# The scan of an RWKV-7 layer on one NeuronCore: group norm statistics, their transposition and two sets of products moved in hand-written queues

## The chip, the cores and the metric

The kernel runs on one core of one Trainium2 chip. The metric is the device time of one execution in microseconds (us). The three runs of the kernel before took 3165.90, 3161.59 and 3163.92 us, with a median of 3163.92 us. TensorE is called PE, its weight loads PEld, VectorE DVE, ScalarE ACT, GpSimd POOL, and the queue that issues the weight DMAs SP.

## The reference

Four transformer blocks of width 1024 over 256 tokens (each a feed-forward, a mixer and another feed-forward) are followed by a fifth block of another design. The mixers of the first and of the fourth block are RWKV-7 time mixes; only these two are touched here. Of such a mixer this is the part that matters:

```python
def step(state, inp):
    r_t, w_t, k_t, v_t, kk_t, a_t = inp
    sa = jnp.einsum('bhvk,bhk->bhv', state, -kk_t)
    state = (state * w_t[:, :, None, :]
             + sa[..., None] * (kk_t * a_t)[:, :, None, :]
             + v_t[..., None] * k_t[:, :, None, :])
    return state, jnp.einsum('bhvk,bhk->bhv', state, r_t)
...
_, y = lax.scan(step, state0, (tm(rh), tm(wh), tm(kh), tm(vh), tm(kk), tm(ah)))
mean = jnp.mean(y, axis=-1, keepdims=True)
var = jnp.mean(jnp.square(y - mean), axis=-1, keepdims=True)
y = ((y - mean) * lax.rsqrt(var + RW_GN_EPS)).reshape(bsz, seq, d) * ln_w + ln_b
out = ((y + bonus.reshape(bsz, seq, d)) * g).astype(h.dtype) @ w_o
```

There are 16 heads of 64 channels. All arithmetic is fp32.

## The kernel before

Each engine has its queue written out by hand in program order, and the queues meet in semaphores. Weights are streamed by SP into a ring of three slots; POOL streams the modulation weights into two buffers, which DVE adds up in pieces of 1.0 or 1.8 us (`beside()`, L505) wherever its queue has one; in the second RWKV layer there are none.

The scan over 256 tokens is done in chunks of 128 tokens, by inverting a triangular matrix per head in levels of 16, 32 and 64 tokens. Its work is cut in four units: unit `u` has chunk `b = u // 2` and head half `u % 2`. An iteration `n` of 1, 2, 3 works on two units at once, the inverse of the head unit `n` and the outputs of the tail unit `n - 1`. PE's queue in an iteration is: `near_again(head)`, `rest(tail)`, `turn_y(head)`, `upper(tail)`, from `n = 2` on `turn_out(n - 2)`, the level 16 product, `across(tail)`, `x32`, `lower(tail)`, `y32`, `state_and_out(tail)`, `level32`, `receptances`, `y64`, `keys` in two halves. `rest`, `upper` are the products of L1631, L1635, L1646 and L1651: first those with all 128 rows of the array (`z.kl` as weights), then, for the second chunk alone (units 2 and 3), those with 64 rows (`z.kk`, `z.r` against the carried state). An fp32 product of this kind stands in the trace as two instructions. Most other products are recorded under L323, the helper `mm`.

DVE masks or adds each product: L2146 and L2160 are the masks of `level16` and `level32`, L2151 and L2156 the sums behind `x32` and `y32`, L2164 is the mask behind `receptances`, L2169 the sum behind `y64`, L2175 the mask behind the two halves of `keys`. `y64` on PE waits for L2160, the second half of `keys` for L2169, `rest` for all of L2175.

Then comes the group norm of the tail unit: `centre` on DVE (L2189, L2190, L2191: sum, mean, subtraction), `spread_read` on ACT (L1902: square), `variance` on DVE (L2196), `deviation` on ACT (L1906: root), `normed` on DVE (L2200, L2202: reciprocal, product). `turn_out` on PE (four transpositions) waits for `normed` by the semaphore `wk_gn`; `out_read` on ACT (L1913) scales what it turned, and `gated` on DVE (L2208, L2209) makes the input of the output projection.

In DVE's queue `centre` stands behind `keys`, at the end of the iteration. In ACT's queue `spread_read` and `deviation` of a unit stand one iteration later than its outputs, around `rest_read` and `x_read`.

Behind the third iteration only unit 3 is left. PE fills the gaps between its steps with `early_outputs(0)` to `(7)`, the output projection of the first chunk, sixteen instructions each; `late_outputs` (L1698) is that of the second chunk.

Of the kernel before, what the change touches and what calls it, by code (L numbers as in the profile page):

```python
# [1224 lines left out]
UNITS = 4  # L1225
# [137 lines left out]
def rw_products(k, pe, pr, j, n):  # L1363
    s, z, tiles = k.sem, RwTiles(k), RwOrder(j, pr.q)
    mm, left = pr.mm, iter(rw_order(j))
# [203 lines left out]
    def near_again(c):  # L1569
        near_product(c.u, 0, k.psum[:, c.bank(0)], None)  # L1570
        near_product(c.u, 1, k.psum[:, c.bank(1)], s["wk_near"])
# [53 lines left out]
    def rest(c):  # L1625
        at("wk_rk_read", c, 1, 2)
        if c.b:
            pe.wait_ge(s["wk_state_read"], 2 * j + c.hf + 1)
        for p in range(4):
            for i in range(2):  # L1630
                ins = part(k.psum[:, c.bank(i), p * 64:(p + 1) * 64], lhsT=z.kl[c.hf][:, 4 * i + p, 1],  # L1631
                           rhs=z.vt[:, c.b, 4 * c.hf + p, z.rows(i)], start=p == 0, stop=c.b == 0, skip_group_check=True)
        for p in range(4 if c.b else 0):
            for i in range(2):
                ins = part(k.psum[:, c.bank(i), p * 64:(p + 1) * 64], lhsT=z.kk[z.rows(i), 4 * c.hf + p, z.now(c.b)],  # L1635
                           rhs=z.state[z.rows(i), 4 * c.hf + p], start=False, stop=True, skip_group_check=True)
        ins.then_inc(s["wk_res"], 1)

    def upper(c):
        at("wk_res_read", c)  # L1640
        for m in range(8):
            mm(k.psum[0:64, c.bank(2), m * 64:(m + 1) * 64], z.y[c.hf][0:64, m, 0:64], z.res[c.hf][0:64, m],
               True, True, s["wk_sa"] if m == 7 else None)
        for p in range(4):
            for i in range(2):
                part(c.out(i, p), lhsT=z.kl[c.hf][:, 4 * i + p, 0], rhs=z.vt[:, c.b, 4 * c.hf + p, z.rows(i)],  # L1646
                     start=p == 0 and (c.b == 1 or i == 0), stop=False, skip_group_check=True)
        if c.b:
            for p in range(4):
                for i in range(2):  # L1650
                    part(c.out(i, p), lhsT=z.r[z.rows(i), 4 * c.hf + p, z.now(c.b)],  # L1651
                         rhs=z.state[z.rows(i), 4 * c.hf + p], start=False, stop=False, skip_group_check=True)

    def across(c):
        at("wk_sa_read", c, 0, 2)
        for m in range(8):
            mm(k.psum[64:P, c.bank(3), m * 64:(m + 1) * 64], z.am[c.hf][0:64, m, 64:P], z.sa[c.hf][0:64, m],
               True, True, s["wk_across"] if m == 7 else None)
# [7 lines left out]
    def state_and_out(c):  # L1666
        at("wk_sa_read", c, 1, 2)
        if c.b == 0:
            for p in range(4):
                for i in range(2):  # L1670
                    o = k.psum[z.rows(i), c.bank(0), p * 64:(p + 1) * 64]
                    mm(o, z.ended_t[0][:, 4 * c.hf + p, z.rows(i)], z.sa[c.hf][:, 4 * i + p], True, False)
                    mm(o, z.ended_t[1][:, 4 * c.hf + p, z.rows(i)], z.vt[:, 0, 4 * c.hf + p, z.rows(i)], False, True,
                       s["wk_state"] if p == 3 and i else None)
        for p in range(4):
            for i in range(2):
                ins = part(c.out(i, p), lhsT=z.rb[c.hf][:, 4 * i + p], rhs=z.sa[c.hf][:, 4 * i + p], start=False,
                           stop=True, skip_group_check=True)
        ins.then_inc(s["wk_out"], 1)

    def turn_out(c):
        at("wk_gn", c)
        for p in range(4):
            pr.turn(k.psum[:, c.turned(), p * P:(p + 1) * P], z.yn_pair[:, p], s["wk_out_turned"] if p == 3 else None)

    def early_outputs(d):
        if d == 0:
            pe.wait_ge(s["rw_gated"], UNITS * j + 2)
        for t in range(KT):
            slot, at = divmod(base + d * KT + t, BLOCKS)  # L1690
            if t == 0:
                pe.wait_ge(k.weights_loaded[slot % RING], 16 * (slot // RING + 1))
            mm(k.psum[:, d // 4 * 2, d % 4 * P:(d % 4 + 1) * P], k.weights[:, slot % RING, at * P:(at + 1) * P],
               z.r[:, t, z.now(0)], t == 0, t == KT - 1)
# [26 lines left out]
    for n in range(1, UNITS):  # L1721
        head, tail = units[n], units[n - 1]
        if head.b:
            pe.wait_ge(s["wk_sa_read"], 2 * (UNITS * j + head.u - 1))
        near_again(head)
        rest(tail)
        turn_y(head)
        upper(tail)
        if n >= 2:
            turn_out(units[n - 2])  # L1730
        if n == 1 and j == 0:
            turn_mod_rows(k, pe, pr, 2)
        level16(head)
        across(tail)
        if n == 1 and j == 0:
            pe.wait_ge(s["mod_ready"], 3)
        x32(head)
        lower(tail)
        y32(head)
        state_and_out(tail)  # L1740
        level32(head)
        receptances(head)
        if n == UNITS - 1:
            early_outputs(0)
        y64(head)
        keys(head)
    tail = units[3]
    early_outputs(1)
    rest(tail)
    early_outputs(2)  # L1750
    upper(tail)
    early_outputs(3)
    turn_out(units[2])
    across(tail)
    early_outputs(4)
    lower(tail)
    early_outputs(5)
    state_and_out(tail)
    early_outputs(6)
    early_outputs(7)  # L1760
    pe.wait_ge(s["rw_gated"], UNITS * j + 3)
    for d in range(KT):
# [27 lines left out]
def rw_act(k, act, ev, j, v_first):  # L1790
# [109 lines left out]
    def spread_read(c):  # L1900
        at("wk_spread_in", c)
        act_(z.sq, z.yn, f.Square).then_inc(s["wk_sq"], 1)  # L1902

    def deviation(c):
        at("wk_var", c)
        act_(z.stat[c.hf][:, 1], z.stat[c.hf][:, 1], f.Sqrt, bias=k.const("gn_eps"), scale=1.0 / 64)\  # L1906
            .then_inc(s["wk_deviation"], 1)
# [10 lines left out]
    for n in range(UNITS + 1):  # L1918
        if n < UNITS:
            near_read(units[n])  # L1920
        if n >= 2:
            spread_read(units[n - 2])
        if n:
            rest_read(units[n - 1])
        if n < UNITS:
            x_read(units[n])
        if n >= 2:
            deviation(units[n - 2])
        if n == 0:
            values_read()  # L1930
            ended_read()
        if n:
            upper_read(units[n - 1])
        if n >= 2:
            out_read(units[n - 2])
        if n:
            lower_read(units[n - 1])
            if units[n - 1].b == 0:
                state_read(units[n - 1])
    spread_read(units[3])  # L1940
    deviation(units[3])
    out_read(units[3])


# [26 lines left out]
def rw_vector(k, dve, own, n, j, q0):  # L1971
# [161 lines left out]
    def open_y(c):  # L2133
        if c.b:
            dve.wait_ge(s["wk_sa"], 2 * (UNITS * j + c.u - 1))
        same = k.const("same16").rearrange("p (c t) -> p c t", t=16)
        for m in range(8):
            i, p = divmod(m, 4)
            ins = v.tensor_tensor(z.y[c.hf][:, m].rearrange("p (c t) -> p c t", t=16),
                                  z.base[:, c.u, 4 * (1 - i) + p:4 * (1 - i) + p + 1].to_broadcast([P, 8, 16]),  # L2140
                                  same, mult)
        ins.then_inc(s["wk_open"], 1)
# [15 lines left out]
    def level32(c):  # L2158
        at("wk_lx", c, 1, 2)
        v.tensor_tensor(z.t[c.hf], c.pair(1), each("level5"), mult).then_inc(s["wk_t"], 1)  # L2160
# [24 lines left out]
    def centre(c):  # L2185
        at("wk_out", c)
        if c.u:
            dve.wait_ge(s["wk_out_turned"], UNITS * j + c.u)
        own.of(v.tensor_reduce(stat(c, 0), c.outs(), AX.X, add))  # L2189
        own.of(v.tensor_scalar(z.stat[c.hf][:, 0], z.stat[c.hf][:, 0], 1.0 / 64, None, mult))  # L2190
        v.tensor_tensor(z.yn, c.outs(), stat(c, 0).unsqueeze(3).to_broadcast([P, 2, 4, 64]), sub)\  # L2191
            .then_inc(s["wk_spread_in"], 1)
# [40 lines left out]
    for n in range(1, UNITS):  # L2233
        head, tail = chunks[n], chunks[n - 1]
        if n == 1 and j == 0:
            mod_columns(k, dve, own, 2)
        level16(head)
        across(tail)
        x32(head)
        y32(head)  # L2240
        beside()
        if n >= 2:
            gated(chunks[n - 2])
        if n + 1 < UNITS:
            open_y(chunks[n + 1])
        level32(head)
        receptances(head)
        y64(head)
        keys(head, 0)
        keys(head, 1)  # L2250
        centre(tail)
        variance(tail)
        normed(tail)
        beside(2)
# [1406 lines left out]
```

## Time and profile before

| | |
|---|---|
| median of three runs | 3163.92 us |
| time of the profiled execution | 3165.9 us |
| its span | 3164.1 us |
| instructions | 49803 |
| PE busy | 3044.1 us, 96% |
| DVE busy | 2373.9 us, 75% |
| ACT busy | 1399.7 us, 44% |
| chain that ended last | PE 85%, DVE 10%, ACT 2%, DMA 2%, issue 1% |
| mean granted TensorE clock | 0.978 |

The span is the time from the first to the last instruction in the profiled execution; the time of a run is a little longer than it. The share of an engine says how long it was occupied in the whole program. The chain that ended last says which engine each moment waited for, followed back from the last instruction. The scan units of the first RWKV layer lie at 419 to 543 us of the span, those of the second at 2306 to 2433 us.

### The profile page before, as it was taken

What the parts mean: (1) busy time and instruction counts of PE and PEld (TensorE: products, weight loads), DVE (VectorE), ACT (ScalarE), POOL (GpSimd) and SP (SyncE); (2) the same over time, 40 slices, a digit from 0 to 9 for tenths busy, and PEclk for the clock granted to TensorE, in tenths of its full rate; (3) what the DMA queues carried; (4) which work ended last, traced back from release to release, by engine and by line L of the source; (5) the groups of instructions that cost most, each with busy time, mean ns of one, the idle gap of its engine ahead of it and who ended that gap; (6) DMA issues with size and microseconds to landing.
All of it is one profiled execution on the core that took longest, in us unless ns stands there. A gap on an engine that the chain in (4) does not pass through costs nothing.

```text
span 3164.1 us, 49803 instructions
## 1 busy us (share of the span) xinstructions
PE 3044.1 (96%) x19866; PEld 2679.8 (85%) x19866; DVE 2373.9 (75%) x3501; ACT 1399.7 (44%) x2222; POOL 97.0 (3%) x187
## 2 busy tenths in 40 slices
PE   7998999999999999999999999999989999999998
PEld 6886789888888988888886888887788888989887
DVE  6978865988877867878867887877754866765685
ACT  4534121544545753545444554534122544465453
POOL 0000000000000000000000000000000000000000
PEclk9999999999999999999999999999999999999899
DMA  8774423676676336675764666662301553443453
GB/s 349 252 287 150 155 100 109 247 269 254 244 264 224 118 119 230 245 283 204 265 236 151 240 260 231 245 244 100 114 1 61 197 183 125 170 167 140 160 182 132
DMA packets 69670, 609.47 MB, mean 193 GB/s; under 512 B 7728, under 2 KB 7888, under 8 KB 31824
## 3 DMA queue, kind: packets, MB, share of 16 engines
q1 hardware_dynamic: 42768, 459.41, 39.1%
q0 software_dynamic: 26352, 144.88, 12.2%
q8 instruction: 158, 2.59, 0.3%
q10 hardware_dynamic: 336, 2.13, 0.2%
q14 instruction: 56, 0.46, 0.0%
HBM read 604.30 MB, written 2.10 MB: 192 GB/s over the span
## 4 chain that ended last, share of the span: by engine, by line
PE 85%; DVE 10%; ACT 2%; DMA 2%; issue 1%; SPq 0%; DVEq 0%; POOLq 0%; ACTq 0%
PE psum L323 26%; PE psum L926 23%; PE psum L930 12%; PE psum L947 10%; PE psum L954 6%; PE psum L321 4%; PE psum L951 2%; PE psum L1698 1%; DVE ada_sum L505 1%; DMA weights<-in_weights 1%; DVE arena L812 1%; DMA ada_in<-in_ada_w 1%; DVE arena L2307 1%; DVE wkv_base L2075 1%; DVE small L2074 1%
## 5 line engine op out<-in xcount | busy, mean ns | idle before, releaser
L877 ACT ACTIVATE unit_high<-weights 128x1024 fp32r<-128x1024 f32 x594 | 628.6, 1060 | 704.7 <-PE psum L930 388.2
L883 DVE TENSOR_TENSOR unit_low<-weights,unit_high 128x1024 fp32r<-128x1024 f32 x594 | 725.5, 1223 | 197.7 <-ACT unit_high L877 197.2
L926 PE MATMUL psum<-h_part,unit_high 128*128 128x512 f32 x3168 | 821.1, 396 | 21.0 <-DVE h_part L799 14.7
L926 PEld LDWEIGHTS psum<-h_part,unit_high 128*128 128x128 f32 x3168 | 576.6, 191 | 129.6 <-issue 17.1
L930 PEld LDWEIGHTS psum<-h_part,unit_low 128*128 128x128 f32 x3168 | 445.6, 192 | 29.5
L930 PE MATMUL psum<-h_part,unit_low 128*128 128x256 f32 x3168 | 466.9, 284 | 0.0
L323 PE MATMUL psum<-in_part,w_part 128*128 128x256 f32 x2784 | 361.3, 290 | 7.2 <-issue 4.8
L323 PEld LDWEIGHTS psum<-in_part,w_part 128*128 128x128 f32 x2784 | 348.4, 196 | 23.1 <-issue 10.8
L947 PE MATMUL psum<-hidden,unit_high 128*128 128x512 f32 x1386 | 353.7, 396 | 0.0
L1053 DVE TENSOR_REDUCE arena<-psum 128x256 f32<-128x512 f32 x396 | 272.7, 689 | 59.1 <-PE psum L930 47.6
L505 DVE SCALAR_TENSOR_TENSOR ada_sum<-ada_in,c_act,ada_sum 128x1536 f32<-128x1536 f32 x154 | 278.6, 1812 | 25.4 <-DMA ada_in<-in_ada_w 25.2
L947 PEld LDWEIGHTS psum<-hidden,unit_high 128*128 128x128 f32 x1386 | 249.2, 189 | 44.2
L323 PE MATMUL psum<-arena,weights 128*128 128x256 f32 (+4 forms) x1360 | 274.2, 374 | 6.6 <-DVE arena L1947 4.3
L323 PEld LDWEIGHTS psum<-arena,weights 128*128 128x128 f32 (+3 forms) x1360 | 216.9, 190 | 60.2 <-issue 27.5
L323 PE MATMUL psum<-arena 128*128 128x128 f32 (+6 forms) x2112 | 231.8, 280 | 22.5 <-DVE arena L2056 7.3
L323 PEld LDWEIGHTS psum<-arena 128*128 128x128 f32 (+3 forms) x2112 | 194.7, 171 | 55.5 <-issue 14.6
L1173 DVE TENSOR_TENSOR w_part<-weights,w_part 128x1024 fp32r<-128x1024 f32 x144 | 175.2, 1221 | 87.6 <-ACT w_part L1167 87.0
L954 PEld LDWEIGHTS psum<-hidden,unit_low 128*128 128x128 f32 x1584 | 214.7, 190 | 13.9
L954 PE MATMUL psum<-hidden,unit_low 128*128 128x256 f32 x1584 | 221.1, 282 | 0.0
L1167 ACT ACTIVATE w_part<-weights 128x1024 fp32r<-128x1024 f32 x144 | 150.9, 1050 | 16.4 <-PE psum L323 16.4
L489 POOL DMA_DIRECT2D ada_in<-in_ada_w x180 | 95.0, 528 | 1976.2 <-DVE ada_sum L505 1461.1
L1018 ACT ACTIVATE hidden<-arena 128x256 fp32r<-128x256 f32 x198 | 82.8, 418 | 89.5 <-DVE arena L1089 73.4
(314 smaller groups left out, 2804.7 us busy)
## 6 DMA issues: line engine op xcount, KB each, us to landing
weights<-in_weights SPq DMA_DIRECT2D x290, 1536.0 KB, 6.5
ada_in<-in_ada_w POOLq DMA_DIRECT2D x182, 768.0 KB, 5.9
consts<-in_consts POOLq DMA_DIRECT2D x1, 1700.0 KB, 16.2
x<-in_x SPq DMA_DIRECT2D x1, 1024.0 KB, 9.2
v_first<-arena ACTq DMA_DIRECT2D x1, 1024.0 KB, 5.0
arena<-v_first ACTq DMA_DIRECT2D x1, 1024.0 KB, 4.8
weights<-in_weights SPq DMA_DIRECT2D x1, 512.0 KB, 5.1
out<-x SPq DMA_DIRECT2D x1, 512.0 KB, 2.6
```

The costliest lines, as they stand in the source:

```text
L321: ins = self.k.nc.tensor.matmul(out, lhsT=w, rhs=x, start=start, stop=stop, skip_group_check=True)
L323: ins = self.k.nc.tensor.matmul(out, lhsT=w, rhs=x, start=start, stop=stop, is_transpose=turn)
L505: ins = k.nc.vector.scalar_tensor_tensor(out, buf, c, out, ALU.mult, ALU.add)
L877: k.nc.scalar.activation(k.unit_part[0][:, n % UNIT_RING], w, ACT.Copy).then_inc(k.sem["unit_high"], 1)
L883: k.nc.vector.tensor_tensor(k.unit_part[1][:, n % UNIT_RING], w, k.unit_part[0][:, n % UNIT_RING].bitcast(FP32), ALU.subtract).then_inc(k. ...
L926: mm(k.psum[:, 2 * (j % 2) + half, :].rearrange("p (i t) -> p i t", i=2), lhsT=part(2 * j + half, 0, t), rhs=k.h_parts[:, :, t], start=t = ...
L930: ins = mm(k.psum[:, 2 * (j % 2) + half, 0:T], lhsT=part(2 * j + half, 1, t), rhs=k.h_part[0][:, t], start=False, stop=t == KT - 1, skip_g ...
L947: mm(k.psum[:, out_bank(d), :].rearrange("p (i t) -> p i t", i=2), lhsT=w, rhs=x, start=f == 0, stop=f == FT - 1, skip_group_check=True)
L954: ins = mm(k.psum[:, out_bank(d), 0:T], lhsT=part(UNITS_UP + v, 1, b), rhs=k.hidden_part[f][:, 0], start=False, stop=f == FT - 1, skip_gro ...
L1053: v.tensor_reduce(to[:, j % RING], k.psum[:, 2 * (j % 2) + half, :].rearrange("p (i t) -> p t i", i=2), AX.X, ALU.add).then_inc(k.sem["gat ...
L1167: self.k.nc.scalar.activation(self.k.w_part[0][:, m % RING], w, ACT.Copy).then_inc(self.k.sem["w_high"], 1)
L1173: self.k.nc.vector.tensor_tensor(self.k.w_part[1][:, m % RING], self.weights(m)[1], self.k.w_part[0][:, m % RING].bitcast(FP32), ALU.subtr ...
```

## The change

Five things are moved; no instruction of arithmetic is added or taken away.

- PE: `turn_out(n - 2)` goes from behind `upper(tail)` to the place right behind `near_again(head)`, ahead of `rest(tail)`.
- PE: in `rest` and `upper` of units 2 and 3 the 64-row products of a pair `p` follow right behind its 128-row products, where before all 128-row products came first. `rest` uses the helper `mm`, and each product opens its own columns.
- PE: behind iteration 3 the order is `rest(3)`, `turn_out(2)`, `early_outputs(0)`, `upper(3)`, and so on; `early_outputs(0)` no longer stands ahead of `y64` in iteration 3, and `early_outputs(6)` goes ahead of `state_and_out(3)`.
- ACT: `spread_read` and `deviation` of a unit go to the end of its own iteration.
- DVE: `centre(tail)` goes ahead of `level32(head)`, and in iteration 3 one more `beside()` stands ahead of it.

```diff
@@ rest(c), PE
         for p in range(4):
             for i in range(2):
-                ins = part(k.psum[:, c.bank(i), p * 64:(p + 1) * 64], lhsT=z.kl[c.hf][:, 4 * i + p, 1],
-                           rhs=z.vt[:, c.b, 4 * c.hf + p, z.rows(i)], start=p == 0, stop=c.b == 0, skip_group_check=True)
-        for p in range(4 if c.b else 0):
-            for i in range(2):
-                ins = part(k.psum[:, c.bank(i), p * 64:(p + 1) * 64], lhsT=z.kk[z.rows(i), 4 * c.hf + p, z.now(c.b)],
-                           rhs=z.state[z.rows(i), 4 * c.hf + p], start=False, stop=True, skip_group_check=True)
-        ins.then_inc(s["wk_res"], 1)
+                mm(k.psum[:, c.bank(i), p * 64:(p + 1) * 64], z.kl[c.hf][:, 4 * i + p, 1],
+                   z.vt[:, c.b, 4 * c.hf + p, z.rows(i)], True, c.b == 0,
+                   s["wk_res"] if p == 3 and i and c.b == 0 else None)
+            if c.b:
+                for i in range(2):
+                    mm(k.psum[:, c.bank(i), p * 64:(p + 1) * 64], z.kk[z.rows(i), 4 * c.hf + p, z.now(c.b)],
+                       z.state[z.rows(i), 4 * c.hf + p], False, True, s["wk_res"] if p == 3 and i else None)
@@ upper(c), PE
-        if c.b:
-            for p in range(4):
+            if c.b:
                 for i in range(2):
                     part(c.out(i, p), lhsT=z.r[z.rows(i), 4 * c.hf + p, z.now(c.b)],
@@ iterations, PE
         near_again(head)
+        if n >= 2:
+            turn_out(units[n - 2])
         rest(tail)
         turn_y(head)
         upper(tail)
-        if n >= 2:
-            turn_out(units[n - 2])
...
         receptances(head)
-        if n == UNITS - 1:
-            early_outputs(0)
         y64(head)
         keys(head)
     tail = units[3]
+    rest(tail)
+    turn_out(units[2])
+    early_outputs(0)
+    upper(tail)
     early_outputs(1)
-    rest(tail)
     early_outputs(2)
-    upper(tail)
+    across(tail)
     early_outputs(3)
-    turn_out(units[2])
-    across(tail)
     early_outputs(4)
     lower(tail)
     early_outputs(5)
+    early_outputs(6)
     state_and_out(tail)
-    early_outputs(6)
     early_outputs(7)
@@ iterations, ACT
             near_read(units[n])
-        if n >= 2:
-            spread_read(units[n - 2])
...
             x_read(units[n])
-        if n >= 2:
-            deviation(units[n - 2])
...
                 state_read(units[n - 1])
-    spread_read(units[3])
-    deviation(units[3])
+            spread_read(units[n - 1])
+            deviation(units[n - 1])
@@ iterations, DVE
             open_y(chunks[n + 1])
+        else:
+            beside()
+        centre(tail)
         level32(head)
         receptances(head)
         y64(head)
         keys(head, 0)
         keys(head, 1)
-        centre(tail)
         variance(tail)
         normed(tail)
         beside(2)
```

## Rows read from the trace of the kernel before

**Rows 1.** The window view: the two stretches in which the scan units run. us, then busy us (x instructions) of PE, PEld, DVE, ACT, POOL, granted clock, DMA share, GB/s.

```profile
419.00:543.00 124.00, 119.30 (x1220) 110.76 (x1219) 75.88 (x111) 24.55 (x46) 5.27 (x10) 1.00 0.19 65
...
2306.00:2433.00 127.00, 123.26 (x1211) 114.86 (x1209) 59.81 (x97) 26.61 (x50) 0.00 (x0) 0.99 0.01 1
```

**Rows 2.** Timeline, second layer, end of unit 1 and first products beside unit 2.

```profile
2338.70 2.61 DVE L2175 TENSOR_TENSOR arena<-psum,consts 128x512 f32<-128x512 f32 x4
...
2338.84 2.57 PE L323 MATMUL psum<-arena 64*128 64x256 f32 x24 [0.25 <-DVE arena L2169]
...
2341.22 0.68 DVE L2189 TENSOR_REDUCE small<-psum 128x8 f32<-128x512 f32 x1
...
2341.36 2.00 PE L1631 MATMUL psum<-arena 128*128 128x64 f32 x16
...
2342.14 0.69 DVE L2191 TENSOR_TENSOR arena<-psum,small 128x512 f32<-128x512 f32 x1
...
2345.32 1.28 ACT L1906 ACT_TABLE_LOAD   x1
...
2347.93 0.82 PE L323 MATMUL psum<-consts,arena 128*128 128x128 f32 x4 [0.69 <-DVE arena L2202]
```

**Rows 3.** Timeline, second layer, group norm of unit 3: variance, root, scaling.

```profile
2421.70 0.69 DVE L2196 TENSOR_REDUCE small<-norm_pair 128x8 f32<-128x512 f32 x1 [0.69 <-ACT norm_pair L1902]
...
2422.42 0.30 ACT L1906 ACTIVATE small<-small,consts 128x8 f32<-128x8 f32 x1 [0.75 <-DVE small L2196]
...
2422.99 0.69 DVE L2202 TENSOR_TENSOR arena<-arena,small 128x512 f32<-128x512 f32 x1
```

**Rows 4.** Timeline, both layers: the second mask (L2160) of iterations 1, 2, 3, and PE behind it.

```profile
447.52 1.23 DVE L2160 TENSOR_TENSOR arena<-psum,consts 128x1024 f32<-128x1024 f32 x1 [1.13 <-PE psum L323]
...
476.01 1.22 DVE L2160 TENSOR_TENSOR arena<-psum,consts 128x1024 f32<-128x1024 f32 x1
...
504.31 1.22 DVE L2160 TENSOR_TENSOR arena<-psum,consts 128x1024 f32<-128x1024 f32 x1
...
504.67 2.05 PE L323 MATMUL psum<-arena,weights 128*128 128x128 f32 x16
...
2363.36 1.22 DVE L2160 TENSOR_TENSOR arena<-psum,consts 128x1024 f32<-128x1024 f32 x1 [0.73 <-PE psum L323]
...
2391.04 1.22 DVE L2160 TENSOR_TENSOR arena<-psum,consts 128x1024 f32<-128x1024 f32 x1 [1.02 <-PE psum L323]
...
2392.02 2.05 PE L323 MATMUL psum<-arena,weights 128*128 128x128 f32 x16
```

**Rows 5.** Timeline, second layer, end of iteration 3.

```profile
2397.04 2.61 DVE L2175 TENSOR_TENSOR arena<-psum,consts 128x512 f32<-128x512 f32 x4
...
2397.18 1.13 PE L323 MATMUL psum<-arena 64*128 64x256 f32 x8 [0.25 <-DVE arena L2169]
...
2398.24 2.05 PE L323 MATMUL psum<-arena,weights 128*128 128x128 f32 x16
```

**Rows 6.** Timeline, second layer: the residual products of unit 2 and what follows.

```profile
2370.53 2.00 PE L1631 MATMUL psum<-arena 128*128 128x64 f32 x16
...
2372.46 0.97 PEld L1635 LDWEIGHTS psum<-arena 64*128 64x128 f32 x16
...
2373.50 1.09 PE L323 MATMUL psum<-consts,arena 128*128 128x128 f32 x8
...
2422.70 3.65 PEld L1698 LDWEIGHTS psum<-arena,weights 128*128 128x128 f32 x32
```

**Rows 7.** Timeline and window view: products with the clock low and high, and a wait ahead of a low clock.

```profile
461.65 2.99 PEld L323 LDWEIGHTS psum<-arena 128*128 128x128 f32 x32
...
2348.33 4.61 PEld L323 LDWEIGHTS psum<-arena 128*128 128x128 f32 x32
...
415.27 2.69 PE L323 MATMUL psum<-consts,arena 128*128 128x128 f32 x16 [2.69 <-DVE arena L2121]
...
416.40:419.80 3.40, 3.40 (x24) 2.94 (x22) 0.00 (x0) 1.90 (x4) 0.00 (x0) 0.51 0.02 6
```

## The prediction

> **What bounds the kernel now.** I read the window view first, for the two stretches that the change touches. In both, PE is busy for all but 4 to 5 us (119.30 of 124, 123.26 of 127) at a granted clock of 1.00 and 0.99, while DVE has 48 and 67 us free [rows 1]. PE sets the end; nothing that only shortens DVE or ACT can pay, and a reordering can win at most PE's few waits. Then I read the timeline for what ends each wait. Beside unit 2 they are: the second half of `keys` waits for the sum L2169, `rest` for the mask L2175 (`near_again` covers all but 0.14), and `turn_out(0)` 0.7 us for the product L2202 of the group norm, whose root came late behind a table load [rows 2]. The first question is thus whether each moved PE step still stands behind what it needs, in DVE's order.
>
> **1. `turn_out` ahead of `rest`.** Its semaphore comes from `normed`. In DVE's new order `normed(n - 2)` still stands behind `keys` of the iteration, and behind it PE has only `near_again` before it now asks for it. In the trace DVE is done with L2175 and free for the next work at 2341.22 (there `centre` starts), and PE starts `rest` at 2341.36 [rows 2]. With `centre` gone from there, `variance` starts at 2341.22. Variance, root, reciprocal and product take 2422.99 + 0.69 - 2421.70 = 1.98 us where nothing else is in the way [rows 3], with 0.05 to reach PE. So `turn_out` starts at 2343.25, 1.9 us later than `rest` does now, and `rest`, `turn_y`, `upper` queue behind it. This happens in iterations 2 and 3. In iteration 2 the present wait of 0.7 goes, as the table load of 1.28 us no longer lies ahead of the root. Per layer 1.9 + 1.9 - 0.7 = 3.1, both layers 6.2 us. ACT's `near_read` now queues behind `deviation` too, but `turn_y`, which wants it, stands behind `turn_out` and `rest`, some 2.4 us of PE work: nothing.
>
> Of the table load the Trainium skill ("ScalarE: Activation LUTs", What ACT_TABLE_LOAD costs) says that it comes with a drain and takes about 2.66 us in all. The trace does not agree: 1.28 us from 2345.32, and the root follows so that L2202's result lets PE start at 2347.93 [rows 2]. I take it as hidden behind unit 0's square; by the page, were it exposed, the sum would be 5 us higher.
>
> **2. `centre` ahead of `level32`.** Its three instructions take 2342.14 + 0.69 - 2341.22 = 1.6 us of DVE [rows 2]. They now stand between PE's product `level32` and its mask L2160, on which `y64` waits. DVE's idle time ahead of L2160 is the only cover. First layer: 1.13 us in iteration 1, so 0.5 is added; none in iteration 2, so 1.6. Second layer: 0.73 in iteration 2, so 0.9 [rows 4]; in iteration 1 I count nothing, since no piece of the modulation sum stands there. Together 3.0 us.
>
> In iteration 3 `early_outputs(0)`, which hid the mask, is gone too. PE is free for `y64` where that product starts now, at 504.67 and 2392.02. In the second layer L2160 would start 1.6 us after DVE came free: 2391.04 - 1.02 + 1.6 = 2391.6, and with 1.22 and 0.05 PE starts at 2392.9: a wait of 0.9. In the first layer DVE has no idle time there, and the new `beside()` of 1.7 us comes on top: 504.31 + 1.6 + 1.7 + 1.27 = 508.9, a wait of 4.2 [rows 4]. Together 5.1 us. The piece of the sum that `beside()` took from the end lay off PE's path: no gain.
>
> **3. `rest(3)` right behind `keys(3)`.** `rest` can start 2.66 us after L2175 starts (2338.70 to 2341.36) [rows 2], so at 2397.04 + 2.66 = 2399.70; PE is free at 2398.24 [rows 5]. Before, `early_outputs(1)` filled this. Wait 1.5, both layers 3.0 us. From there on PE had no wait before and has none after; the early outputs are the same work elsewhere, so the moves of (1) to (7) count nothing. `late_outputs` wait for `gated(2)` and `gated(3)`, which come as many steps ahead of PE as before.
>
> Waits so far: 6.2 + 3.0 + 5.1 + 3.0 = 17.3 us.
>
> **4. 64-row products between 128-row products.** No product is added. In the long run a 128-row instruction takes (3.65 - 0.19) / 31 = 0.112 us. The sixteen of L1631 should take 1.79; from their start to that of L1635 it is 1.93 us: 0.14 more. The sixteen of L1635 run in pairs, seven steps in 0.97 - 0.19 = 0.78, so eight in 0.89; to the next product it is 1.04: 0.15 more [rows 6]. So each change between 128 and 64 rows costs about 0.145 us. `rest` now has seven changes inside where it had one, and so has `upper`: 6 x 0.145 = 0.87, for `rest` and `upper`, two units, two layers: 8 x 0.87 = 7.0 us, all on PE's path. Bounds: the row shows one change after sixteen instructions, not one after four. If PE could look past short blocks it would be 0; twice the price, 14, if each block also lost its pairing. I take the price of the row, as the pairs of L1635 work on two blocks of rows and two pairs stand in each block now.
>
> The Trainium skill ("TensorEngine Tiling (Array Packing)", Tiling Modes) says that changing the tiling mode drains the engine. By that rule the price recurs at every change, which is 7.0 as above; if it held only for the first, it would be nothing.
>
> **5. The clock.** The same 32 loads stand in the trace once in 2.99 us and once in 4.61 [rows 7]: a stretch at 1.2 GHz in place of 2.4 costs 1.6. The stretch at clock 0.51 from 416.40 follows a wait of 2.69 us, that of 2348 follows the wait of `turn_out(0)` in the second layer, only 0.7 long [rows 2, 7]. The new waits of 1.9 to 4.2 us are of the size of the first. Candidates: in the first layer `turn_out` twice, `y64` in iterations 2 and 3 with `rest(3)` close behind it; in the second layer `turn_out` twice and `rest(3)`, less the one that is there. Six, of which I count five: 8 us. Bounds: 0, if short waits between much work leave the clock alone, and eight such stretches, 13.
>
> **Sum.** 17.3 + 7.0 + 8 = 32.3 us: span 3164.1 + 32.3 = 3196.4. The profiled execution's own time is 3165.9, 2 above the median; against the median 3163.9 + 32.3 = 3196.
>
> **Rivals.**
> - The changes of rows cost nothing (4 is zero): 3189. For it: the row shows one change only. Against: both directions cost.
> - The clock holds: 3188. For it: unit 2 of the first layer has the same 0.7 us wait with no fall (2.99 us) [rows 7]. Against: the new waits are thrice as long.
> - The table load waits for DVE together with the root. ACT would carry 1.28 us more behind `variance(0)`, in both layers: 2.6 more, 3199. For it: it stands directly ahead of L1906. Against: the load is an instruction of its own, and nothing in the source gives it a wait.
> - Not slower: DVE gets ahead. The change takes `centre` off the stretch between `keys` and `normed`. If `wk_gn` came before `near_again` ends, the waits of `turn_out` (2 x 0.7) and the low clock in the second layer (1.6) would go: 3 us less, 3161, if DVE were so far ahead that it covered the other places as well. The point from which it decides is 1.9 us of DVE time per iteration; `centre` gives back only 1.6, and that 1.6 is put in ahead of a mask which PE waits for. In iteration 3 of the first layer it would need 4.2.
>
> **How the numbers follow.** Forecast with waits, changes and some low clock 0.60; changes free 0.13; clock holds 0.12; table load exposed 0.05; DVE ahead or the places cancel 0.10. The range reaches from both bounds at zero, less some waits that overlap (3164 + 17.3 = 3181, down to 3178), to 3164 + 17.3 + 14 + 13 = 3208. Faster and slower are counted from 0.2%, 6.3 us, about what a measurement of this kernel can tell. The last case is split: faster 0.05, same 0.05; slower 0.90.
>
> **What would show it.** PE idle just ahead of the four transpositions behind `near_again`, ended by L2202, about 2 us each; L2160 ending PE's idle time ahead of `y64` in iteration 3, 4 us in the first layer; idle time ahead of L1631 in the tail, 1.5 us; `rest(2)` from first to last product 3.8 us in place of 2.97; more stretches with clock 0.5 between 455 and 560. The forecast is wrong if `turn_out` finds its semaphore set, or if the pairs p follow each other at 0.112 us throughout.

## The result and the profile after

The changed kernel takes 3224.65 us (median of four runs, 3219.76 to 3228.61) beside 3162.76 us: a ratio of 1.0184, with a 95% interval of 1.017 to 1.0199. It is 58 us slower by the ratio and 62 by these medians; the median of all 37 timed executions of the changed kernel on record is 3220.51 us. 3196 was forecast, with a range up to 3208: the direction is right, the forecast is about half of the change, and the time lies outside the range. The profiled execution took 3215.61 us, with a span of 3213.9 us and a mean granted clock of 0.969; the median clock of the 37 is 0.966. In what follows, one execution of experiment 11's kernel, 3775.27 us at a mean granted clock of 0.744, is left out of its ratio.

The window view of the changed kernel over the same work as [rows 1], and over parts of it: the first wait of `turn_out`, around which the clock stays high, then the time from unit 2 on, and stretches at the low clock. The columns are start:end, length, busy time and instructions of PE, PEld, DVE, ACT and POOL, granted clock, DMA share, GB/s.

```profile
core 0: us, PE busy (x) PEld busy (x) DVE busy (x) ACT busy (x) POOL busy (x), PEclk, DMA share, GB/s
416.00:573.00 157.00, 142.12 (x1211) 130.26 (x1208) 76.94 (x111) 24.54 (x46) 5.81 (x11) 0.85 0.17 56
441.00:476.00 35.00, 29.77 (x308) 27.43 (x307) 24.55 (x43) 8.33 (x14) 2.11 (x4) 1.00 0.27 91
476.30:548.00 71.70, 63.71 (x406) 56.77 (x407) 31.23 (x34) 8.90 (x18) 3.17 (x6) 0.69 0.20 67
486.50:507.00 20.50, 20.50 (x107) 17.94 (x107) 2.92 (x3) 3.60 (x7) 1.06 (x2) 0.50 0.23 78
544.50:551.30 6.80, 6.80 (x34) 6.45 (x34) 0.00 (x0) 0.00 (x0) 0.00 (x0) 0.50 0.00 0
2335.00:2485.00 150.00, 140.54 (x1212) 129.19 (x1211) 59.47 (x97) 26.61 (x50) 0.00 (x0) 0.89 0.00 1
2374.00:2452.00 78.00, 72.20 (x554) 65.27 (x554) 30.77 (x46) 12.13 (x23) 0.00 (x0) 0.78 0.00 1
2374.10:2384.30 10.20, 10.20 (x56) 9.75 (x55) 0.00 (x0) 3.60 (x7) 0.00 (x0) 0.50 0.01 2
2408.20:2425.30 17.10, 17.10 (x90) 15.11 (x90) 0.00 (x0) 3.60 (x7) 0.00 (x0) 0.50 0.00 1
```

The first layer's stretch lengthened from 124 to 157 us, the second's from 127 to 150, with nearly the same instructions of PE (1211 and 1212, where [rows 1] have 1220 and 1211: the windows' edges cut off a few). PE's busy time went up by 142.12 - 119.30 = 22.8 and by 140.54 - 123.26 = 17.3 us, its idle time by 10.2 and 5.7. The clock fell from 1.00 to 0.85 and from 0.99 to 0.89; between 476 and 548 us it is 0.69. The longest low stretch runs from 486.5 to 507: a clock of 0.50, and PE busy for all of its 20.50 us.

Eight low stretches begin in the two scans. In the first layer they are 3.4, 20.5, 6.8, 10.2 and 6.8 us long (from 476.3, 486.5, 520.6, 530.9 and 544.5), in the second 10.2, 17.1 and 6.9 us (from 2374.1, 2408.2 and 2445.7): 82 us in all. Seven of them begin at one of the waits below or up to 3 us behind it. The one at 544.5 begins among the mixed products of `upper(3)`, with no wait above 0.25 us in the 14 us ahead.

Now the waits, in the timeline of the first layer. What stands in brackets is the time that the engine was idle before, and who released it. DVE's and ACT's lines have other numbers than in the kernel before, lower by up to six: L2154, L2155 and L2159 are the mask behind `level32` (before L2160), L2169 and L2174 the mask behind `keys` (L2175), L2196, L2197 and L2201 the product of `normed` (L2202).

```profile
444.84 1.28 ACT L1904 ACT_TABLE_LOAD   x1
...
445.34 3.12 PE L323 MATMUL psum<-arena 128*128 128x128 f32 x24 [0.53 <-DVE arena L2154]
...
453.12 0.66 PE L323 MATMUL psum<-consts,arena 128*128 128x128 f32 x4 [1.84 <-DVE arena L2196]
...
476.31 4.68 PE L323 MATMUL psum<-arena 128*128 128x128 f32 x24 [2.66 <-DVE arena L2154]
...
521.79 6.64 PE L323 MATMUL psum<-arena 128*128 128x128 f32 x32 [4.10 <-DVE arena L2154]
...
530.15 6.23 PE L323 MATMUL psum<-arena 128*128 128x64 f32 x32 [1.72 <-DVE arena L2169]
```

Each wait is where the prediction has it, and within 0.3 us as long as it says: `turn_out(0)` behind `near_again` 1.84 us, released by L2196, which is `normed`; `y64` released by L2154, the mask of `level32`, 0.53, 2.66 and 4.10 us in iterations 1, 2 and 3 (before 0.23, 1.14 and none; 0.5 and 1.6 more and 4.2 were forecast); `rest(3)` 1.72 us where 1.5 was forecast. In the second layer, by the timeline, `turn_out` waits 1.84 us twice, `y64` 0.23, 0.93 and 0.64, and `rest(3)` 1.39. The table load at 444.84 starts right behind the square of unit 0 and is done long before the root: it is hidden, as step 1 took it.

The row changes in `upper`, at the low clock (496 us) and at the high one (542 us):

```profile
496.15 1.11 PE L1646 MATMUL psum<-arena 128*128 128x64 f32 x4
...
497.20 0.69 PE L1650 MATMUL psum<-arena 64*128 64x64 f32 x4
...
497.82 1.11 PE L1646 MATMUL psum<-arena 128*128 128x64 f32 x4
...
541.96 0.66 PE L1646 MATMUL psum<-arena 128*128 128x64 f32 x4
...
542.55 0.44 PE L1650 MATMUL psum<-arena 64*128 64x64 f32 x4
...
542.92 0.66 PE L1646 MATMUL psum<-arena 128*128 128x64 f32 x4
```

At the high clock a pair takes 542.92 - 541.96 = 0.96 us; four would take 3.84, where [rows 6] have 2.97 for the four together: 0.87 more, the forecast of step 4. In the second layer all four pairs of `upper(3)` run at the high clock and take 2457.70 - 2453.88 = 3.82 us. The Trainium skill ("TensorEngine Tiling (Array Packing)", Tiling Modes) says that every change of the tiling mode drains the engine. The trace agrees: the pairs of `upper(3)` in the second layer begin 0.95, 0.96 and 0.96 us apart, so the price recurs from pair to pair. At the low clock a pair takes 1.67 us.

What was missed is thus neither a wait nor a row change. PE's busy time grew by 22.8 + 17.3 = 40.1 us, of which the row changes are 7 by the price above; the other 33 are put down to the low clock, where I had reckoned 8. The clocks of the two stretches say much the same. A mean clock of 0.85 is reached with 0.15 x 2 of the time at half speed: 157 x 2 x 0.15 = 47 and 150 x 2 x 0.11 = 33 us ran at 1.2 GHz, 80 in all, which by the 1.6 us for 3.4 of [rows 7] would cost 38, an estimate.

### The profile page after: what moved, and what is told of

Same layout as the page of the kernel before. It is cut to its first block, busy times and chain, and to the rows that moved or that the text cites. A ratio compares the mean times of both kernels' runs of the same rounds, so it can differ in the third digit from the quotient of the medians.

```text
span 3213.9 us, 49803 instructions
## 1 busy us (share of the span) xinstructions
PE 3077.8 (96%) x19866; PEld 2706.3 (84%) x19866; DVE 2373.2 (74%) x3501; ACT 1399.8 (44%) x2222; POOL 97.0 (3%) x187
## 4 chain that ended last, share of the span: by engine, by line
PE 84%; DVE 11%; ACT 2%; issue 1%; DMA 1%; SPq 0%; DVEq 0%; POOLq 0%; ACTq 0%
PE psum L323 26%; PE psum L926 23%; PE psum L930 12%; PE psum L947 10%; PE psum L954 6%; PE psum L321 4%; PE psum L951 1%; PE psum L1697 1%; DVE ada_sum L505 1%; DMA weights<-in_weights 1%; DVE arena L812 1%; PE psum L1646 1%; DVE arena L2303 1%; DVE wkv_base L2069 1%; DVE small L2068 1%
## 5 line engine op out<-in xcount | busy, mean ns | idle before, releaser
L323 PE MATMUL psum<-arena 64*128 64x128 f32 (+7 forms) x2304 | 272.7, 293 | 32.1 <-DVE arena L2154 9.1
L323 PEld LDWEIGHTS psum<-arena 64*128 64x128 f32 (+3 forms) x2304 | 231.0, 183 | 70.1 <-issue 15.3
```

The source lines that it names most:

```text
L323: ins = self.k.nc.tensor.matmul(out, lhsT=w, rhs=x, start=start, stop=stop, is_transpose=turn)
```

## The experiments

Each time stands beside the kernel before on the same chip; the ratio has its 95% interval behind it. "Worth" is the ratio's distance from 1 times 3162 us. A trace is one execution and can be far from its kernel's median: that of experiment 1 took 3215.55 us, the longest of its four, that of experiment 2 3174.50, the shortest of its four.

### Experiment 1: all moves, without the row changes

```diff
 def rest(c), def upper(c):   # in the changed kernel
-    128-row products of p, 64-row products of p, next p
+    all 128-row products, then all 64-row products
```

> The changed kernel with the 64-row products of `rest` and `upper` back behind all 128-row products; every other move stays. The waits of 17 us stay too. Theory 1 (the mixed rows are what holds TensorE's clock at 1.2 GHz for 10 to 20 us behind each wait, where a dense stretch lets it rise at once): the low stretches of units 2 and 3 shrink to 3 to 7 us each, and the time is 3163 + 17 + some 6 = 3186. Theory 2 (the waits alone bring the clock down, and the mixed rows cost only their 7 us): 3224 less 7 and what these 7 cost at the low clock, about 3212.

Measured: 3206.95 us, ratio 1.0132 (1.0098 to 1.0167): worth 42 us. That is neither 3186 nor 3212, but it shows that the low clock comes without the added row changes. The window view before, at and behind `turn_out(0)` in the first layer, behind `turn_out(1)`, and behind both in the second layer:

```profile
430.00:455.80 25.80, 22.84 (x243) 21.00 (x242) 16.46 (x30) 5.64 (x8) 0.53 (x1) 1.00 0.09 32
455.80:469.50 13.70, 13.70 (x71) 13.25 (x72) 2.55 (x2) 3.60 (x7) 1.06 (x2) 0.50 0.35 116
469.50:482.00 12.50, 12.25 (x143) 11.50 (x143) 8.42 (x13) 0.98 (x2) 0.53 (x1) 1.00 0.06 9
496.80:510.50 13.70, 13.70 (x85) 12.78 (x86) 1.11 (x1) 3.60 (x7) 1.06 (x2) 0.51 0.32 116
2374.10:2387.80 13.70, 13.70 (x73) 13.25 (x72) 0.00 (x0) 3.60 (x7) 0.00 (x0) 0.51 0.00 1
2411.70:2432.20 20.50, 20.50 (x122) 19.24 (x122) 1.92 (x2) 3.60 (x7) 0.00 (x0) 0.50 0.00 1
```

And the timeline of the first of them:

```profile
455.75 1.11 PE L323 MATMUL psum<-consts,arena 128*128 128x128 f32 x4 [1.84 <-DVE arena L2197]
...
456.65 3.52 PE L1631 MATMUL psum<-arena 128*128 128x64 f32 x16
...
467.17 4.13 PE L323 MATMUL psum<-arena 128*128 128x128 f32 x32
```

The clock is 1.00 up to the wait of 1.84 us, falls with it, and stays at 0.50 for 13.7 us, through `rest`, `turn_y`, `upper` and the level 16 product, though PE has no idle time in them (13.70 of 13.70). I had priced a fall after a wait at 1.6 us. It costs about 6.5 here: 13.7 us, at 1.6 for each 3.4 [rows 7].

The wait does not bring the clock down each time. In the changed kernel PE has the same queue up to this place and the same wait of 1.84 us, at 453.12, and its clock stays at 1.00 (441 to 476 us above). Of the eight such waits in these two traces seven were followed by a low stretch. What decides it isn't shown; a single stretch of one trace proves little, and the counts and the medians have to carry the argument.

### Experiment 2: the row changes alone

```diff
 # in the kernel before
-    all 128-row products, then all 64-row products
+    128-row products of p, 64-row products of p, next p
```

> The kernel before, with the mixed rows of `rest` and `upper` alone. Theory 1 in its strong form (mixed rows bring the clock down by themselves): low stretches appear at `rest` and `upper` of units 2 and 3 with no new wait ahead of them, 7 us of row changes and 10 to 25 us of low clock, 3180 to 3195. In its weak form (they only keep down a clock that a wait brought down), and by theory 2: 3163 + 7 = 3170, the clock at 1.00 as before.

Measured: 3181.28 us, ratio 1.0063 (1.0042 to 1.0085): worth 20 us, of which the row changes are 7. The rest is more than the weak form allows. The window view of the profiled execution, unit 2 of the first layer and what follows its `rest(3)`, then `rest(2)` of the second layer and what follows:

```profile
483.00:512.00 29.00, 28.51 (x267) 25.77 (x268) 18.23 (x19) 4.87 (x10) 1.59 (x3) 1.00 0.25 82
516.30:519.70 3.40, 3.40 (x19) 3.29 (x18) 2.32 (x3) 0.79 (x2) 0.00 (x0) 0.50 0.00 0
2374.00:2383.00 9.00, 9.00 (x86) 7.82 (x85) 3.81 (x8) 3.94 (x6) 0.00 (x0) 1.00 0.01 2
2383.30:2390.10 6.80, 6.80 (x35) 6.22 (x35) 0.08 (x1) 1.50 (x4) 0.00 (x0) 0.51 0.00 0
```

In the first layer the clock stays at 1.00 through the mixed products of unit 2, and falls for 3.4 us right behind those of `rest(3)` (512.65 to 516.4), with no wait above 0.25 us in the 40 us ahead. In the second it falls at 2383.3, among the mixed products of `upper(2)`, for 6.8 us, and in the 14 us ahead PE waited nowhere longer than 0.25 us. So mixed rows can bring it down, but don't each time.

### Experiment 3: `turn_out` back behind `upper`

```diff
 # in the changed kernel
         near_again(head)
-        if n >= 2:
-            turn_out(units[n - 2])
         rest(tail)
         turn_y(head)
         upper(tail)
+        if n >= 2:
+            turn_out(units[n - 2])
```

> The changed kernel with `turn_out(n - 2)` back behind `upper(tail)`. The wait of 1.84 us ahead of `rest(1)` and `rest(2)` goes in both layers, 4 x 1.9 less 2 x 0.1 for the wait on L2169's successor: 7 us less. If the wait brings the clock down in `rest(2)` (theory of the wait plus mixed rows), the low stretches of 20.5 and 17.1 us behind it go as well, up to 18 us more: 3200. If the mixed rows do that alone, the low stretches stay and it is 3217.

Measured: 3192.05 us, ratio 1.0096 (1.0074 to 1.0117): worth 30 us, so 28 less than the changed kernel. The wait itself is a quarter of this; the forecast of 3200 was too careful. Low stretches are still there over the mixed rows of unit 2: in the first layer from the end of `rest(2)` to `turn_out(1)`, in the second from the middle of `upper(2)`:

```profile
486.20:499.90 13.70, 13.70 (x74) 12.19 (x75) 1.74 (x2) 3.72 (x7) 1.06 (x2) 0.51 0.32 115
2397.70:2404.50 6.80, 6.80 (x38) 6.22 (x37) 0.40 (x1) 1.51 (x4) 0.00 (x0) 0.51 0.00 0
```

The wait for `normed` ahead of them is gone, and the stretches are 13.7 us instead of 20.5 and 6.8 instead of 17.1. The first begins at the end of the mixed `rest(2)` (480.12 to 486.7); the nearest wait above 0.25 us, 2.66 us for L2154, ended 9 us before, at 476.76, and the clock was 1.00 from there to 480. As in experiment 2, the mixed rows are the likelier cause: in the traces of the kernels with grouped rows, each fall in the scans comes within some 3 us of the end of a wait of 0.69 us or more.

### Experiment 4: the table load early

```diff
 # in the kernel before, ScalarE
             lower_read(units[n - 1])
             if units[n - 1].b == 0:
                 state_read(units[n - 1])
+            if n == 1:
+                root_table(k)   # one small root, loads the table
```

> The kernel before, with one small root on ScalarE behind `lower_read(0)`, so that the table load of 1.28 us falls into ScalarE's idle time in iteration 1. If the load is what makes `turn_out(0)` late: PE's wait of 0.7 us goes in both layers, and with it perhaps the low clock of 3.4 us in the second one (1.6): 1.4 to 3 us less, 3160 to 3162. The rival is that the load is redone ahead of the root anyway, or that another step is late in its place: no change.

Measured: 3157.58 us, ratio 0.9992 (0.9981 to 1.0003). The timeline, first layer:

```profile
438.08 1.28 ACT L662 ACT_TABLE_LOAD   x1
...
452.45 0.29 ACT L1906 ACTIVATE small<-small,consts 128x8 f32<-128x8 f32 x1
...
454.33 0.61 PE L323 MATMUL psum<-consts,arena 128*128 128x128 f32 x4
```

The load falls into ACT's idle time, the root follows its variance at once, and `turn_out(0)` no longer waits.

### Experiments 5 and 6: the same wait, filled

```diff
+            pe.wait_ge(s["wk_state_read"], 2 * j + units[n - 2].hf + 1)
+            for _ in range(8):
+                part(k.psum[:, units[n - 2].turned(), 0:P], lhsT=k.const("ident"), rhs=k.const("ident"), start=True,
+                     stop=True, skip_group_check=True)
             turn_out(units[n - 2])
```

Experiment 5 adds this to the kernel of experiment 1, experiment 6 to the changed kernel. The loop issues sixteen instructions; `turn_out` writes over what they leave.

> The changed kernel with grouped rows (as in the first experiment), and PE's wait ahead of `turn_out` filled with eight throwaway products of 128x128 by 128 columns, sixteen instructions or 1.9 us, whose output `turn_out` overwrites. The moment at which `turn_out` may start stays the same. Theory 1 (idle time brings the clock down and the work behind it is slow to bring it back): the stretches of 14 to 20 us at 1.2 GHz behind `turn_out` go, four of them, 62 us of low clock at 1.6 per 3.4 us: up to 29 us less than 3207, so 3178 to 3188. Theory 2 (the products of `rest`, `turn_y` and `upper` bring the clock down themselves, whatever stands ahead of them): no change, 3207.

> The changed kernel itself, with mixed rows, and the same sixteen throwaway instructions in the wait ahead of `turn_out`. Theory 1: the low stretches in `rest(2)` and `upper(2)` go, 38 us of low clock or more, 18 us less, plus what follows: 3200 to 3205. If the mixed rows bring the clock down by themselves, the stretches start inside `rest(2)` all the same and the time stays over 3215.

Measured: 3185.49 us, ratio 1.0065 (1.0041 to 1.0088), and 3204.43 us, ratio 1.0116 (1.0082 to 1.0149). Work that is of no use makes the kernels 21 and 20 us faster, and the intervals lie apart from those of experiment 1 and of the changed kernel. This is the experiment that tells the two apart, the wait and the clock, since the transpositions start when they did: 1.91 us behind the start of the filling, and 454.74 - 450.33 = 4.41 us behind that of `near_again`, where experiment 1 has 455.75 - 451.33 = 4.42.

```profile
452.83 2.05 PE L1729 MATMUL psum<-consts 128*128 128x128 f32 x16
...
454.74 0.66 PE L323 MATMUL psum<-consts,arena 128*128 128x128 f32 x4
...
455.24 1.90 PE L1631 MATMUL psum<-arena 128*128 128x64 f32 x16
```

The window view of experiment 5, before and behind `turn_out(0)`, at the wait for the mask of `level32` that was not filled, then from the filling ahead of `turn_out(1)` on in both layers:

```profile
430.00:452.80 22.80, 21.68 (x226) 20.01 (x226) 14.86 (x27) 3.48 (x5) 0.53 (x1) 1.00 0.10 36
452.80:475.50 22.70, 22.22 (x237) 20.96 (x236) 13.43 (x21) 5.78 (x11) 1.58 (x3) 1.00 0.26 83
478.90:482.30 3.40, 3.40 (x19) 3.00 (x18) 1.21 (x2) 0.00 (x0) 0.00 (x0) 0.55 0.00 0
484.90:505.00 20.10, 19.76 (x201) 18.55 (x200) 9.31 (x10) 5.39 (x10) 1.05 (x2) 1.00 0.23 80
2386.40:2405.00 18.60, 18.36 (x189) 17.28 (x188) 4.67 (x7) 5.39 (x10) 0.00 (x0) 1.00 0.00 1
```

The stretch that had 0.50 for 13.7 us in experiment 1 now has 1.00 throughout, and the clock falls first at the 2.7 us wait that is left. At the eight filled places of experiments 5 and 6 the clock is 1.00 through the filling, `turn_out` and `rest`; at the eight unfilled ones of experiment 1 and the changed kernel it fell seven times. In experiment 6 it falls for 6.8 us at 496.0, in the mixed `upper(2)` of the first layer, and not in the other three units that follow a filling. The prediction's steps had the idle time right, and this shows what the idle time does. The Trainium skill ("TensorE: Matmul & The Clock Gate", Part 1) says that the throttled state is the default and activity releases it. The trace agrees in this: throwaway activity was enough to keep 1.00 over the 22.7 us of the second window.

### Experiments 7 and 8: the two other moves alone

```diff
 # 7, in the kernel before, VectorE
             open_y(chunks[n + 1])
+        else:
+            beside()
+        centre(tail)
         level32(head)
...
         keys(head, 1)
-        centre(tail)
 # 8, in the kernel before, PE
-        if n == UNITS - 1:
-            early_outputs(0)
...
+    rest(tail); turn_out(units[2]); early_outputs(0); upper(tail) ...
```

> The kernel before with `centre` ahead of `level32` on DVE and the extra `beside()`, alone. By the prediction's step 2: 0.5 + 1.6 + 0.9 us for the mask L2160, and in iteration 3 of the first layer 508.9 less the end of `early_outputs(0)` at 506.5, 2.4 us, none in the second: 5.4 us of waits. If short waits cost only themselves: 3168. If a wait of 2.4 to 2.9 us also brings the clock down for 3.4 to 7 us: up to 3175.

> The kernel before with PE's new order behind iteration 3, alone. Waits: `rest(3)` 1.5 in both layers; the mask L2160 ahead of `y64` in iteration 3 0.4 to 0.9: 4 to 5 us, 3167. With a low stretch behind `rest(3)` in each layer, 1.6 to 5 us more each: 3170 to 3177.

Measured: 3165.44 us, ratio 1.0007 (0.9992 to 1.0022), and 3174.55 us, ratio 1.0029 (1.0015 to 1.0043): worth 2 and 9 us. The waits came nearly as reckoned, and the low clock behind those of experiment 7 is 3.4 us in its trace. `centre` alone, ahead of `y64` in iteration 3 of the first layer:

```profile
509.01 2.25 PE L323 MATMUL psum<-arena 128*128 128x128 f32 x15 [2.12 <-DVE arena L2160]
```

The new order behind iteration 3 alone, `rest(3)` and `turn_out(2)`:

```profile
505.36 2.00 PE L1631 MATMUL psum<-arena 128*128 128x64 f32 x16 [1.39 <-DVE arena L2174]
...
510.48 1.12 PE L323 MATMUL psum<-consts,arena 128*128 128x128 f32 x4 [1.84 <-DVE arena L2201]
```

The second wait, 1.84 us for `normed(2)`, I had left out of the expectation: alone, without `centre` moved, the group norm comes later. In the changed kernel it isn't there.

Three moves put alone into the kernel before are worth 20 (row changes), 9 (order behind iteration 3) and 2 (`centre`): 31, beside the 30 of experiment 3's kernel, which has these three and ACT's move. Putting `turn_out` ahead of `rest` on top costs the other 28. With 4 to 7 us of uncertainty on each, that adds up; neither `turn_out` in the kernel before nor ACT's move was run alone. In the changed kernel the row changes are worth 16 (its ratio less that of experiment 1), in the kernel before 20.

### Experiments 9 to 11: a kernel that gains

```diff
 # experiment 9, at the end of norm_products, with experiment 4's edit
+    if n < NORMS and SUBS[n] == "ffn":
+        for _ in range(6 if after_ffn(n) else 13):
+            k.nc.tensor.matmul(k.psum[:, 0, 0:P], lhsT=k.const("ident"), rhs=k.const("ident"), ...)
 # experiment 11
-        for _ in range(6 if after_ffn(n) else 13):
+        for _ in range(6 if after_ffn(n) else 13 if SUBS[n - 1] == "rwkv" else 0):
```

> The kernel before with the early table load of the fourth experiment, and with throwaway products of 128x128 by 128 columns in PE's wait ahead of each feed-forward but the first: six (1.3 us), after an RWKV, Mamba or attention layer thirteen (2.9 us). In the trace of before, 3.4 to 13.7 us at 1.2 GHz begin with these waits, some 35 us in all, worth up to 16 us. If idle time ahead of them is the cause: half of it or more is saved, 8 to 16 us, and 3 to 5 us by the table: 3141 to 3152. If the clock falls whatever is in the wait: 3158, as with the table alone, or more where the products hold up the first real one.

> The fourth experiment again, with more rounds: 3158, 0.1 to 0.2% under the kernel before, if the wait for the table load is what was saved; within 0.05% if the first measurement was chance.

> The ninth experiment with no throwaway products behind the Mamba and the attention layer, where PE's wait ahead of the feed-forward is 0.4 us and not 2.9, so that thirteen of them held up the first real product by some 2 us each. If that is why the ninth kernel gained nothing over the early table load: 4 us less than 3158, 3154. If it stays at 3158, the clock ahead of the feed-forwards isn't worth what was reckoned.

Measured: 3158.30 us, ratio 0.9988 (0.9976 to 0.9999); 3157.59 us, 0.9992 (0.9982 to 1.0001); 3154.18 us, 0.9981 (0.9971 to 0.9991). The early table load gives 0.1% both times, but both intervals just take in 1. In its second profile the second layer's scan has the full clock:

```profile
2300.00:2427.00 127.00, 123.88 (x1227) 115.59 (x1224) 60.92 (x100) 26.23 (x51) 0.00 (x0) 1.00 0.04 14
```

Experiment 9, forecast at 3141 to 3152, gained nothing on top. Experiment 11 drops the filling where there was nearly no wait to fill (0.4 us), and its kernel is 5 to 6 us under the kernel before, the lowest ratio of all that ran. The interval excludes 1; that it beats experiments 4 and 9 is not shown, as their intervals overlap with it. The timeline and the window view of experiment 11 behind the second RWKV layer,

```profile
2433.20 4.69 PE L777 MATMUL psum<-consts 128*128 128x128 f32 x26
...
2437.65 0.47 PE L930 MATMUL psum<-h_part,unit_high 128*128 128x512 f32 x1
```

```profile
2430.00:2470.00 40.00, 39.38 (x232) 35.18 (x232) 34.16 (x54) 25.32 (x38) 0.00 (x0) 0.96 0.57 217
```

beside the same work in the kernel before, which runs 9.8 us later there:

```profile
2448.36 0.77 PE L926 MATMUL psum<-h_part,unit_high 128*128 128x512 f32 x1 [3.51 <-DVE h_part L799]
```

```profile
2439.80:2479.80 40.00, 35.87 (x187) 31.54 (x187) 31.54 (x49) 23.12 (x35) 0.00 (x0) 0.83 0.52 199
```

PE waited 3.5 us there and ran with a clock of 0.83 in these 40 us; filled, it is 0.96. With the early table load alone (experiment 10, 2429 to 2469 us) it is 0.87.

## Why the prediction was half right

1. **`turn_out` ahead of `rest`** (6.2 us): right in place, releaser and length, 1.84 us of idle time. As priced it is less than a quarter of what the move costs on top of the others, 28 us.
2. **`centre` ahead of `level32`, `beside()`** (8.1 us with iteration 3): the waits were 2.66 and 4.10 us for L2154, as reckoned. Alone the move costs 2 us within an interval of -3 to +7; there `early_outputs(0)` stays in place and covers part of the wait in iteration 3 (2.12 us in place of 4.10).
3. **`rest(3)` behind `keys(3)`** (3.0 us): 1.72 and 1.39 us idle.
4. **Row changes** (7.0 us): 0.87 us in `upper` at the high clock. The price is right; what the prediction left out is that with mixed rows the clock also falls in places without a wait (experiments 2 and 3). Alone the move is worth 20 us, 13 more than its price.
5. **The clock** (8 us): this is the term that was mis-sized, and the step that failed. "Six, of which I count five: 8 us" priced each fall at one stretch of 3.4 us, as long as the one of 2348.33 in [rows 7], which ran into dense 128-column products. The places were right: seven of the eight low stretches begin at waits that the step names as candidates. Their length was not. Behind the four waits of `turn_out` they were 20.5, 10.2 and 17.1 us long and once absent, in experiment 1 13.7 us three times and 20.5; 13.7 us cost 6.5 and 20.5 cost 9.6 at 1.6 per 3.4. The eighth, among mixed rows, no candidate covered. Measured: 82 us at 1.2 GHz and some 33 us lost in the two scans. That there were eight, the number of the upper bound, is luck: the bound of 13 us took each at the shortest length, which would make 27 us of low clock.

Idle time 16 (17.3 forecast), changes 7 and clock 33 make 56 us in the two stretches of the profiled execution. Its span grew by 49.8, since outside the two stretches the traced execution is 6.2 us shorter than that of the kernel before; no instruction was changed there. It is also shorter than the 3220.51 us of the median execution, whose clock is lower (0.966 in place of 0.969). That the longer executions lose the rest to the clock fits these numbers; no trace of one was taken.

Of the rivals, the table load that waits fell (444.84), free row changes fell (0.96 us a pair), DVE ahead fell. "The clock holds" fell too (0.85 and 0.89).

Why the clock takes 10 to 20 us to rise behind some waits and 3.4 behind others, and why it doesn't fall at all behind some of the same length (453.12 in the changed kernel), is not settled. That the work behind the wait has few columns (64 in `rest` and `upper`, 64x64 in parts of `upper`) and that it rose each time near the 128-column products of the next levels fits the stretches shown here, but I didn't isolate it: it is argued, not shown. Shown is that without the idle time the low stretches behind `turn_out` go (experiments 5 and 6) and that the row changes cost more than their price (16 us by the ratios between experiment 1 and the changed kernel, 16 between 5 and 6, 20 in the kernel before, for 7 us of changes). That this surplus is low clock rests on the traces of experiments 2, 3 and 6 and on the stretch at 544.5.

## What to carry to other kernels

Don't price a new wait on TensorE by its own length alone: here 1.84 us of idle time ahead of small products was followed by 10 to 20 us at the low clock in seven of eight places, 5 to 10 us lost each. If a wait can't be avoided, put independent dense products into it; throwaway ones paid here, and the early outputs did that service in the kernel before: moving them away cost 9 us (experiment 8). Keep products of one row mode together.

## What the runs showed of the hardware

- Throwaway products in four waits of 1.8 to 2.2 us made the kernel 21 us faster (3206.95 to 3185.49 us), and the clock stayed at 1.00 there.
- The same wait of 1.84 us behind the same work was followed by 13.7 us at 1.2 GHz in one trace (experiment 1, 455.8 us) and by none in another (changed kernel, 453.12 us).
- The clock can stay at 1.2 GHz for 20.5 us while PE is busy the whole time, and mixed 128-row and 64-row products seem to bring it down by themselves: with no wait above 0.25 us in the 9 us ahead in one place (486.2 us in experiment 3), in the 14 us ahead in another (2383.3 us in experiment 2) and in the 40 us ahead in a third (516.3 us in experiment 2), though not in each place (experiment 2, 483 to 512 us: 1.00).
- Each change between 128-row and 64-row products costs 0.145 us at the high clock, also after blocks of only four instructions (a pair of blocks took 0.96 us, where 2.97 / 4 = 0.74 were needed without the added changes).
